# Eight steps of the search for the largest index scores, moved from the attention into the feature stage, and index units dealt out anew

## What is computed

```python
def dsa_mixer(q, k, v, q_idx, k_idx, w_idx, cos_h, sin_h, cos_i, sin_i):
    ...
    n_top = min(DSA_TOPK, S // 4)
    ...
        rel = jax.nn.relu(jnp.einsum('bqhd,bsd->bqhs', qi, k_idx).astype(jnp.float32))
        score = jnp.einsum('bqh,bqhs->bqs', wi, rel)
        score = jnp.where(k_pos[None, None, :] <= q_pos[None, :, None], score, NEG_INF)
        _, idx = lax.top_k(score, n_top)
        ...
        s = jnp.einsum('bqhd,bqkd->bhqk', qb, kg).astype(jnp.float32) * scale
        p = masked_softmax(s, (idx <= q_pos[None, :, None])[:, None])
```

## Time and profile before

| | us |
|---|---|
| median of 3 runs | 3346.08 |
| lowest and highest | 3340.59, 3346.92 |
| span of the profiled execution | 3349.0 |
| TensorE busy in it | 3244.9 |
| VectorE busy in it | 1487.5 |
| ScalarE busy in it | 1272.6 |
| GpSimd busy in it | 384.3 |

### The profile page before, as it was taken

How to read it: one execution, slowest core, us unless ns; L and a number is a source line. 1 busy time by engine, 2 the same in 40 slices (tenths; PEclk the granted TensorE clock), 3 DMA queues, 4 the chain that set the end, 5 groups by cost and what they waited for, 6 DMA issues and landing times. The chain is left out here.

```text
span 3349.0 us, 37289 instructions
## 1 busy us (share of the span) xinstructions
PE 3244.9 (97%) x14860; PEld 2566.0 (77%) x14860; DVE 1487.5 (44%) x2324; ACT 1272.6 (38%) x2190; POOL 384.3 (11%) x277
## 2 busy tenths in 40 slices
PE   9999999999999999999979999999999998899998
PEld 7767678878888888877656888878887766578886
DVE  4154523244243333355875533343334478563333
ACT  3344643233232223235655423242222456542222
POOL 0411324410000000002510000000000243000000
PEclk9998999999999999999989999999999999999999
DMA  4211213323333333332001232323332310023332
GB/s 154 88 44 38 88 58 106 96 87 95 101 95 99 96 99 92 99 104 88 26 1 63 88 96 93 100 87 96 95 95 88 129 45 1 27 88 95 97 94 74
DMA packets 76061, 276.92 MB, mean 83 GB/s; under 512 B 8688, under 2 KB 8944, under 8 KB 75632
## 3 DMA queue, kind: packets, MB, share of 16 engines
q1 hardware_dynamic: 75888, 274.54, 26.5%
HBM read 272.41 MB, written 2.10 MB: 82 GB/s over the span
## 5 line engine op out<-in xcount | busy, mean ns | idle before, releaser
L545 ACT ACTIVATE w_hi<-raw_slabs 128x1024 fp32r<-128x1024 f32 x489 | 516.7, 1057 | 1236.5 <-PE ps L585 1128.8
L560 DVE TENSOR_TENSOR w_lo<-raw_slabs,w_hi 128x1024 fp32r<-128x1024 f32 x372 | 454.8, 1223 | 717.3 <-ACT w_hi L545 717.2
L585 PE MATMUL ps<-in_hi,w_hi 128*128 128x512 f32 x1840 | 719.5, 391 | 5.0 <-DVE in_lo L911 5.0
L585 PE MATMUL ps<-in_hi,w_lo 128*128 128x512 f32 x1840 | 716.3, 389 | 0.0
L585 PE MATMUL ps<-in_lo,w_hi 128*128 128x512 f32 x1840 | 716.2, 389 | 0.0
L585 PE MATMUL ps<-parts,w_hi 128*128 128x512 f32 x2240 | 693.9, 391 | 0.9 <-DVE scratch L1528 0.8
L560 POOL TENSOR_TENSOR w_lo<-raw_slabs,w_hi 128x1024 fp32r<-128x1024 f32 x117 | 287.7, 2461 | 2315.2 <-ACT w_hi L545 2298.1
L585 PEld LDWEIGHTS ps<-parts,w_hi 128*128 128x128 f32 x2240 | 420.5, 188 | 92.6 <-issue 4.3
L585 PE MATMUL ps<-parts,w_lo 128*128 128x512 f32 x1120 | 436.0, 389 | 0.0
L585 PEld LDWEIGHTS ps<-in_hi,w_hi 128*128 128x128 f32 x1840 | 345.5, 188 | 83.2 <-DVE in_lo L911 9.2
L585 PEld LDWEIGHTS ps<-in_lo,w_hi 128*128 128x128 f32 x1840 | 345.5, 188 | 72.0 <-issue 1.0
(11 more groups left out here) (303 smaller groups left out, 3579.4 us busy)
## 6 DMA issues: line engine op xcount, KB each, us to landing
raw_slabs<-weights SPq DMA_DIRECT2D x503, 512.0 KB, 3.6
big<-rope SPq DMA_DIRECT2D x2, 2304.0 KB, 8.8
x_resid<-xT SPq DMA_DIRECT2D x8, 256.0 KB, 5.0
outT<-x_resid SPq DMA_DIRECT2D x8, 256.0 KB, 2.0
const_cols<-consts SPq DMA_DIRECT2D x1, 836.0 KB, 9.6
scratch<-brow SPq DMA_DIRECT2D x1, 768.0 KB, 9.4
vector_cols<-vec SPq DMA_DIRECT2D x2, 45.5 KB, 9.9
vector_cols<-vec SPq DMA_DIRECT2D x1, 68.5 KB, 3.1
```

Source lines behind the costliest of these rows:

```text
L545: self.nc.scalar.activation(self.w_hi[:, m % SPLIT, :], self.raw[:, n % RAW, :], ACT.Copy)\
L560: (self.nc.gpsimd if i is None else self.nc.vector).tensor_tensor(self.w_lo[:, m % SPLIT, :], self.raw[:, n % RAW, :], self.w_hi[:, m % SP ...
L585: mm = k.nc.tensor.matmul(out, lhsT, rhs, start=(c == 0 and m == 0), stop=(last and m == 2))
```

## The change

The first 8 of the 48 steps of each layer leave the first attention and stand in the feature stage: 1 behind job 10, 2 each behind jobs 11, 12 and 13, 1 behind job 14, on VectorE after all else that `Features` has there. The attention spreads the 36 that are left over its 65 passes. The index units are dealt out as 3, 3, 2 (the first query block) behind jobs 7 to 9 and 3, 4, 4, 3, 2 behind jobs 10 to 14. `EARLY` is 8, so that all units of the first block use banks 6 and 7.

```diff
-TOP_CUTS = (0, 32, 44)
+TOP_CUTS = (8, 32, 44)
...
-    RING, EARLY = 4, 6
+    RING, EARLY = 4, 8
...
     def bank(self, i):
-        at = 6 + i % 2 if i < self.EARLY else (3, 6, 7)[i % 3]
+        at = 6 + i % 2 if i < self.EARLY else (3, 6, 7)[(i - self.EARLY) % 3]
...
-    UNITS = {**{7 + n: range(2 * n, 2 * n + 2) for n in range(3)}, 10: range(6, 9), **{11 + n: range(4 * n + 9, 4 * n + 13) for n in range(3)}, 14: range(21, 24)}
+    UNITS = {7: range(0, 3), 8: range(3, 6), 9: range(6, 8), 10: range(8, 11), 11: range(11, 15), 12: range(15, 19), 13: range(19, 22), 14: range(22, 24)}
     CMP, KV = 3, 7
-    STEPS = {}
+    STEPS = {10: 1, 11: 2, 12: 2, 13: 2, 14: 1}
```

## The result

The changed kernel takes 3364.11 us (median of 4 runs, 3357.58 to 3368.15), the kernel before 3343.34 us over its 4 runs: a ratio of 1.0064, 95% interval [1.0048, 1.0080]. A second series gave 3358.90 against 3340.22 us, 1.0054 [1.0042, 1.0066]. The forecast was 3353.0 us in a range of 3340 to 3360, so the time lies above the range. The likeliest case had +6.9 us; the two series show 20.8 and 18.7 us.

The account below looks back on a forecast made before the run. TensorE was taken to bound the kernel, busy nearly throughout. Per layer, features +5.0, attention -2.5 and clock +0.9 made +3.4 us, +6.9 for both: 3353.0 us, range 3340 to 3360.

Parts of the forecast that it names:

- The likeliest case: Whole kernel: +3.4 us per layer, +6.9 us for both, so runs should show 3353.0 us; chance 0.46.
- Job 7 and job 8 on TensorE: Features: late third index units at jobs 7 and 8 delay TensorE's start of the norm's sums by 3.3 us.
- The step at job 10 in the wait of 2.96 us: Features, VectorE: the step and the moved index unit fit in its wait for TensorE, costing 0.
- The price of a step: VectorE: each 256-wide step holds it 0.86 us, also beside GpSimd; eight make 6.9 us per layer.
- The first rope of the tail: Features, VectorE: job 14's rope begins 6.2 us later, at 1600.3, with the waits before it gone.
- 1.2 us come back: End of the features: ropes clear of GpSimd's L2754 run faster and return about 1.2 us, leaving +5.0 per layer.
- The attention: First attention: 36 steps instead of 44 shorten it by 2.5 us per layer, between 1.6 and 6.9.
- The clock: Break between features and attention: the stall may bring another clock fall; half its 1.7 us counted, +0.9 per layer.
- The sum: Per layer 5.0 - 2.5 + 0.9 = +3.4 us, both +6.9 us, giving 3353.0 us.
- The rival with a new fall of the clock: Clock falls again in each layer, features cost 6.2: +8.0 us per layer, 3362 us; chance 0.10.
- That the backlog hides: Features: rope 14 starts before about 1597, features cost 2.4 us; -4.5 per layer, 3337 us; chance 0.14.
- That the attention gives all 6.9 us back: Attention: all 6.9 us of moved step time return, -1.0 us per layer, 3344 us, no visible change; chance 0.30.

Follow-up runs that it names:

- 40 steps: Kernel before with four steps moved, one each behind jobs 10 to 13, the other 40 spread evenly over the attention: ratio 0.9983 [0.9974, 0.9992].
- other slots: Changed kernel with its 36 attention steps in the slots they have when 40 are spread over the 65: ratio 1.0037 [1.0022, 1.0051].
- the filler in the stall: Changed kernel plus eleven useless products on TensorE in its wait ahead of job 16's rotation: ratio 1.0031 [1.0019, 1.0043].
- free banks: Changed kernel with the rotations of jobs 16 and 17 in banks 7 and 6, which the index has left: ratio 1.0015 [1.0006, 1.0024].

## Why the prediction was wrong, step by step

- **Job 7 and job 8 on TensorE: +3.3 us.** Measured +3.16 (the norm's sums at +9.76 instead of +6.60). Right; the wait is 1.68 us ahead of the third unit.
- **The step at job 10 in the wait of 2.96 us: nothing.** Right: VectorE still waits 2.21 us there, and even three steps are free.
- **The price of a step, 0.86 us, beside GpSimd too.** Right: two steps that lie beside L2754 have a MAX8 of 0.43 us each. (GpSimd does not work all the time in the attention, as the prediction has it, but for about half of it.)
- **The first rope of the tail: +6.2 us, and no waits between jobs 11 and 14.** Measured +6.97; no waits. Right, 0.8 short.
- **1.2 us come back.** The size is right, the reason is not. VectorE's ropes did end only 5.6 us later, clear of GpSimd; but TensorE is released by the first instruction of rope 14, for job 16, ahead of all that. What came back is its own old wait of 1.40 us ahead of job 17. At full clock the features cost +5.2 and +4.6 us, forecast +5.0.
- **The attention: -2.5 us per layer.** This step failed: -0.2 and -0.6. The prediction spread the gain over thirds of the attention by the number of steps in each, and left out what stands behind the last row maximum and what the clock does inside this stage. Up to the last row maximum 1.4 and 1.2 us were won, by the change and by leaving the eight steps out alike; behind it they were lost. Over the whole kernel leaving out eight steps is worth nothing at full clock (+0.7 us, standard error 0.6). That 2.7 and 2.1 us came with 40 steps, and 1.5 and 4.2 with other slots, owes more to the clock than to the steps. Why the last evictions come no sooner is not shown.
- **The clock: +0.9 us per layer, half of one fall.** Mis-sized: 7.7 us for both layers together by the runs, 3.9 each, all of which the filler in the stall took away. The stall of 4 to 5 us was forecast rightly (4.83), and the end of the range for its price, +3.4, was nearer than the value taken: in the features alone it is 1.7 and 3.4 us.
- **The sum.** Forecast +6.9 us. Measured: 10.0 at full clock and 7.7 for the clock, 17.7 by the means of the second series. Two terms failed in the same direction, the attention by some 2.1 us per layer, the clock by 3.0. The rival with a new fall of the clock, features at 6.2 and little back from the attention, gave 3362 us and had a chance of 0.10; it came nearest, though its features were too dear and its attention too good. The range, too, ended below it.
- **The rivals that gave more back.** That the backlog hides was to be decided at 1597 us on the clock of the trace of before (+56.2 us); the rope came at +60.3, and the rival fell as said. That the attention gives all 6.9 us back fell by the run without the eight steps.

Open: where the 2 to 3 us of the clock's price outside the features' tail lie; why the clock falls less often in the attention with some slots than with others; and what holds up the attention's end behind the last row maximum.

## What to carry to other kernels

Work that is spread over slots by a formula moves as a whole when its amount changes, and its places can matter more than its amount: try the same amount in other slots before you believe a price per piece. Split every gain and loss into time at full clock and cost of the clock before you explain it; here most of what looked like the slots' doing was the clock. An engine that is late at the end of a stage is paid for twice, with the stall and here also with the clock behind it; ask which buffer the other engine waits for (here free banks took over two thirds of the loss away) before moving more work there. And fill a wait up to its length: three steps in a wait of 2.96 us were free, one step each behind four jobs cost 0.4 us of features, all eight 5.2 to 6.1.

## What the runs showed of the hardware

- A stall of TensorE of 4.8 to 5.2 us was followed by a fall to 1.2 GHz that cost 1.7 to 3.4 us, in ten out of ten cases (five profiles, two layers); waits of 1.4 us were followed by none ahead of the attention, nor was a stall of 5.3 us with 3.1 us of useless products in it.
- A fall can come without a stall: from 252 to 272 us the kernel before had TensorE busy throughout and a granted clock of 0.50 to 0.70 (8.6 us), in one profile, and the first profile of the changed kernel 1.00 there.
- The same attention costs 5.1 us of clock in layer 0 and 8.5 in layer 1 of the kernel before, and 0.0 to 10.2 us in the kernels with other steps or slots.
- The fillers, eleven products of 128x512, took 3.11 us, 0.28 each, where the page has 0.391 for the kernel's own of that shape; why was not looked into. They lay in a wait that was there anyway, so the 3.1 us of work per layer cost 1.3 us at full clock for the whole kernel (3321.7 against 3320.4) and saved 8.0 us of the clock (29.6 against 37.6, measured in different series).
